# The levels of a DeltaNet scan on four 64x64 tiles of TensorE, in two PSUM banks, with two products and the turns placed elsewhere

## The reference, cut to what matters

```
a_strict = jnp.where(strict, einsum('bhnid,bhnjd->bhnij', k, k) * decay * beta[..., :, None], 0.0)
rhs = jnp.concatenate([k * (beta * jnp.exp(gc))[..., None], v * beta[..., None]], axis=-1)
sol = lax.linalg.triangular_solve(a_strict, rhs, left_side=True, lower=True, unit_diagonal=True)
```

## Time and profile before

| | us |
|---|---|
| Median of 3 runs | 4400.55 (4396.9 to 4403.37) |
| Profiled execution | 4417.49 |
| Its span in the trace | 4415.8 |
| TensorE busy, matmuls | 4001.1 (91%) |
| DVE busy | 2326.8 (53%) |
| ACT busy | 1489.9 (34%) |
| POOL busy | 608.8 (14%) |
| Granted clock of TensorE, mean | 0.96 |

### The profile page before, as it was taken

The page is one execution under the profiler, slowest core; times in us unless marked ns, Lnnn a source line. Parts: engine busy times, 40 slices in busy tenths (PEclk is TensorE's granted clock), DMA queues, the critical chain, the costliest instruction groups (busy, mean ns, idle before and its releaser), DMA issues. The chain is left out here.

```text
span 4415.8 us, 107674 instructions
## 1 busy us (share of the span) xinstructions
PE 4001.1 (91%) x46477; PEld 3548.8 (80%) x46477; DVE 2326.8 (53%) x4078; ACT 1489.9 (34%) x2670; POOL 608.8 (14%) x755
## 2 busy tenths in 40 slices
PE   6999989999958888999998999989999768888998
PEld 5899977897738886899998999967997568867886
DVE  4555556454474434665556555563554564345434
ACT  4333343333252222433234333343332532223222
POOL 1221200331001100121211212100330010100000
PEclk8999999999979999999999999999999789999999
DMA  5433331000200003223223333321002000012332
GB/s 200 129 113 100 101 100 53 21 2 19 61 1 4 4 4 101 81 87 95 88 70 110 101 112 116 111 67 43 3 2 79 0 3 4 4 64 77 105 96 76
DMA packets 409088, 288.04 MB, mean 65 GB/s; under 512 B 13438, under 2 KB 366180, under 8 KB 408164
## 3 DMA queue, kind: packets, MB, share of 16 engines
q1 hardware_dynamic: 408676, 281.86, 20.9%
HBM read 270.27 MB, written 11.53 MB: 64 GB/s over the span
## 5 line engine op out<-in xcount | busy, mean ns | idle before, releaser
L793 ACT ACTIVATE w_hi<-w_raw 128x512 fp32r<-128x512 f32 (+1 forms) x724 | 405.4, 612 | 647.9 <-POOL w_raw L777 339.5
L800 DVE TENSOR_TENSOR w_lo<-w_raw,w_hi 128x512 fp32r<-128x512 f32 (+1 forms) x724 | 478.4, 701 | 173.9 <-ACT w_hi L793 173.9
L908 PE MATMUL PS<-x_hi,w_hi 128*128 128x384 f32 x1680 | 562.3, 335 | 0.4 <-DVE hid_flat L1089 0.4
L908 PE MATMUL PS<-x_lo,w_hi 128*128 128x384 f32 x1680 | 561.3, 334 | 0.0
L908 PE MATMUL PS<-x_hi,w_lo 128*128 128x384 f32 x1680 | 561.2, 334 | 0.0
L1174 DVE SCALAR_TENSOR_TENSOR arena<-PS,mod,arena 128x256 f32<-128x256 f32 (+1 forms) x336 | 198.3, 632 | 340.7 <-PE PS L921 340.7
L1089 DVE TENSOR_TENSOR hid_flat<-hid_flat,PS 128x384 f32<-128x384 f32 (+1 forms) x454 | 246.7, 557 | 247.4 <-PE PS L908 156.0
L921 PE MATMUL PS<-hidden_hi,w_hi 128*128 128x256 f32 (+1 forms) x1232 | 341.8, 347 | 7.6 <-DVE hidden_lo L1141 5.7
L921 PE MATMUL PS<-hidden_lo,w_hi 128*128 128x256 f32 (+1 forms) x1232 | 336.8, 343 | 0.0
L921 PE MATMUL PS<-hidden_hi,w_lo 128*128 128x256 f32 (+1 forms) x1232 | 336.7, 343 | 0.0
L908 PEld LDWEIGHTS PS<-x_hi,w_hi 128*128 128x128 f32 x1680 | 315.4, 188 | 0.7 <-DVE hid_flat L1089 0.7
(11 more groups left out here) (361 smaller groups left out, 8360.1 us busy)
## 6 DMA issues: line engine op xcount, KB each, us to landing
w_raw<-in_ffn_w_dram SPq DMA_DIRECT2D x512, 256.0 KB, 4.0
arena<-in_ada_w_dram SPq DMA_DIRECT2D x120, 512.0 KB, 5.9
arena<-in_w_in_dram SPq DMA_DIRECT2D x64, 512.0 KB, 4.0
arena<-in_ada_w_dram SPq DMA_DIRECT2D x6, 2048.0 KB, 14.0
arena<-in_w_out_dram SPq DMA_DIRECT2D x16, 512.0 KB, 3.8
h_save<-arena SPq DMA_DIRECT2D x16, 384.0 KB, 2.5
arena<-h_save SPq DMA_DIRECT2D x2, 3072.0 KB, 14.7
w_raw<-in_ffn_w_dram SPq DMA_DIRECT2D x32, 128.0 KB, 2.3
```

Source lines behind the costliest of these rows:

```text
L793: nc.scalar.activation(w_hi[:, high_place(n, what, j), 0:size], w_raw[:, load_of[what] % 2, place, 0:size], ACT.Copy).then_inc(w_high_read ...
L800: nc.vector.tensor_tensor(w_lo[:, b, place, 0:size], w_raw[:, b, place, 0:size], w_hi[:, high_place(n, what, j), 0:size].bitcast(F32), ALU ...
L908: mm = pe.matmul(PS[:, 4 * b + bank, 0:half], w[wo], x_split[xo][:, j, k, 0:half], start=(k == 0 and q == 0), stop=(k == KH - 1 and q == 2))
```

## The change

- `times` and the product of the lower part go through `FOUR_TILES`: the order of heads is 0, 2, 1, 3, each with both halves. Heads 0 and 1 land where they did. Heads 2 and 3 land in the other half of the partitions (`lands`), so that their matmuls use the two off-diagonal 64x64 tiles of the array. Two swaps in a level bring X back to its own half.
- A group's result lies in two banks, 256 columns per head (`two_banks`, `level_blocks`): heads 0 and 1 in the first, 2 and 3 in the second. The product of the lower part goes to banks 4g and 4g + 1, the turn of X and the product with TP to 4g + 2 and 4g + 3. The last turn of X isn't spread over four tiles and goes to bank 4g + 2.
- Since bank 4g + 3 is now used in the levels, DVE's product with `begc` (AV) moves in front of all levels, directly behind ATTN of the same group, and the first turn of X waits for ATTN and AV.
- The order in a level is now, for each group, the turn of X and then the lower part times X; then for each group X times TP. The turn had been the last phase of a level.
- Before the first turn TensorE does five matmuls of 128x128 on the identity into a bank that nobody reads (`keep_busy`), and two more before the first turn of group 1.

```diff
--- before.py
+++ after.py
@@ -1595,10 +1595,6 @@
             v = t.rearrange(f"{axes} (b s j) -> {axes} b s j", s=2, j=1 << l)
             return v[:, :, :, 0, :] if axes == "p u" else v[:, :, 0, :]
 
-        def packed(t, l):
-
-            return t.rearrange("p (u b j) -> p u b j", u=4, j=1 << l)
-
         def blocks(b, p=slice(0, P)):
             return PS[p, b, 0:256].rearrange("p (u t) -> p u t", u=DN_H)
 
@@ -1715,13 +1711,27 @@
                 with pool.Fori(1 if first == 0 else 0, steps) as i:
                     step(first, a, w, i, True)
 
+
+
+
+        ACROSS = {0: HALVES[1], 64: HALVES[0]}
+        FOUR_TILES = [(u, p) for pair in ((0, 2), (1, 3)) for u in pair for p in HALVES]
+
+        def lands(u, p):
+            return p if u < 2 else ACROSS[p.start]
+
+        def two_banks(b, w):
+            return PS[:, b:b + 2, :].rearrange("p a c -> p (a c)").rearrange("p (u c) -> p u c", u=DN_H)[:, :, 0:w]
+
+        def level_blocks(b, l):
+            return two_banks(b, 32).rearrange("p u (b j) -> p u b j", j=1 << l)
+
         def pe_dn(pe, layer):
 
             def times(b, width, lhs, rhs):
 
-                for u in range(DN_H):
-                    for p in HALVES:
-                        mm = pe.matmul(PS[p, b, u * width:(u + 1) * width], lhs(u, p), rhs(u, p), start=True, stop=True)
+                for u, p in FOUR_TILES:
+                    mm = pe.matmul(two_banks(b, width)[lands(u, p), u], lhs(u, p), rhs(u, p), start=True, stop=True)
                 return mm
 
             def spread_gates(it):
@@ -1769,29 +1779,50 @@
                         turn(4 * g, DM[g]).then_inc(at_turned[g], 1)
                     n = LEVELS_DN - 1
                     xs, ts, yt = XS * layer + n * (first + i), TS * layer + n * (first + i), y_count(layer, first + i)
-                    for l in range(n):
-                        if l > 0:
-                            for g in range(2):
-                                c = 4 * g
-                                pe.wait_ge(x_ready[g], xs + l)
-                                for u in range(DN_H):
-                                    for p in HALVES:
-                                        mm = pe.matmul(packed(PS[p, c + 1, 0:128], l)[:, u], AT[g][p, u, p],
-                                                       even(XP[g][p, u, :], l, "p"), start=True, stop=True)
-                                mm.then_inc(tx_summed[g], 1)
-                            for g in range(2):
-                                c = 4 * g
-                                pe.wait_ge(tx_masked[g], ts + l)
-                                pe.wait_ge(y_ready[g], yt + l)
-                                if l == 1:
-                                    pe.wait_ge(attn_ready[g], it + 1)
-                                times(c + 2, 32, lambda u, p: YP[g][p, u, :], lambda u, p: TP[g][p, u, :]).then_inc(xd_summed[g], 1)
+                    def turn_x(g, l):
+                        pe.wait_ge(x_ready[g], xs + l + 1)
+                        if l == 0:
+                            pe.wait_ge(attn_ready[g], it + 1)
+                            pe.wait_ge(kst_ready[g], own + 1)
+                        if l < n - 1:
+                            mm = times(4 * g + 2, 64, lambda u, p: XP[g][p, u, :], lambda u, p: id_c[p])
+                        else:
+                            for u in range(DN_H):
+                                for p in HALVES:
+                                    mm = pe.matmul(blocks(4 * g + 2, p)[:, u], XP[g][p, u, :], id_c[p], start=True, stop=True)
+                        mm.then_inc(x_turned[g], 1)
+
+                    def lower_times_x(g, l):
+                        pe.wait_ge(x_ready[g], xs + l)
+                        if l == 1:
+                            pe.wait_ge(at_moved[g], it + 1)
+                        for u, p in FOUR_TILES:
+                            mm = pe.matmul(level_blocks(4 * g, l)[lands(u, p), u], AT[g][p, u, p],
+                                           even(XP[g][p, u, :], l, "p"), start=True, stop=True)
+                        mm.then_inc(tx_summed[g], 1)
+
+                    def x_times_lower(g, l):
+                        pe.wait_ge(tx_masked[g], ts + l)
+                        pe.wait_ge(y_ready[g], yt + l)
+                        times(4 * g + 2, 32, lambda u, q: YP[g][q, u, :], lambda u, q: TP[g][q, u, :]).then_inc(xd_summed[g], 1)
+
+
+
+                    def keep_busy(g, times):
+                        for _ in range(times):
+                            pe.matmul(PS[:, 4 * g + 1, 0:P], ident[:, :], ident[:, :], start=True, stop=True)
+
+                    keep_busy(0, 5)
+                    for l in range(1, n):
                         for g in range(2):
-                            c = 4 * g
-                            pe.wait_ge(x_ready[g], xs + l + 1)
-                            if l == 0:
-                                pe.wait_ge(at_moved[g], it + 1)
-                            times(c, 64, lambda u, p: XP[g][p, u, :], lambda u, p: id_c[p]).then_inc(x_turned[g], 1)
+                            if l == 1 and g == 1:
+                                keep_busy(1, 2)
+                            turn_x(g, l - 1)
+                            lower_times_x(g, l)
+                        for g in range(2):
+                            x_times_lower(g, l)
+                    for g in range(2):
+                        turn_x(g, n - 1)
                     lo, hi = HALVES
                     for g in range(2):
                         for u in range(DN_H):
@@ -1854,10 +1885,10 @@
                             if l > 0:
                                 act.wait_ge(xd_summed[g], TS * layer + n * (first + i) + l)
                             if l < n - 1:
-                                ins = sc.activation(YP[g], blocks(4 * g), ACT.Copy)
+                                ins = sc.activation(YP[g], two_banks(4 * g + 2, 64), ACT.Copy)
                             else:
                                 for p in HALVES:
-                                    ins = sc.activation(Y[g][p, :, p], blocks(4 * g, p), ACT.Copy)
+                                    ins = sc.activation(Y[g][p, :, p], blocks(4 * g + 2, p), ACT.Copy)
                             ins.then_inc(y_ready[g], 1)
                     lo, hi = HALVES
                     for g in range(2):
@@ -1907,22 +1938,20 @@
                         dve.wait_ge(kq_ready[g], it + 1)
                         dve.wait_ge(at_turned[g], it + 1)
                         v.tensor_tensor(ATTN[g], DMT[g], bank(4 * g + 2), ALU.mult).then_inc(attn_ready[g], 1)
+                        u = slice(g * DN_H, (g + 1) * DN_H)
+                        row = lambda t: bc(t[:, bass.ds(first + i, 1), u].rearrange("p o u -> p (o u)"), 2, [P, DN_H, P])
+                        dve.wait_ge(ks_ready[g], it + 1)
+                        v.tensor_tensor(AV[g], bank(4 * g + 3), row(begc), ALU.mult).then_inc(kst_ready[g], 1)
                     for l in range(1, n):
                         for g in range(2):
                             dve.wait_ge(tx_summed[g], TS * layer + n * (first + i) + l)
-                            v.tensor_tensor(TP[g].rearrange("p u (b j) -> p u b j", j=1 << l), packed(PS[:, 4 * g + 1, 0:128], l),
+                            v.tensor_tensor(TP[g].rearrange("p u (b j) -> p u b j", j=1 << l), level_blocks(4 * g, l),
                                             level_mask(l), ALU.mult).then_inc(tx_masked[g], 1)
                         for g in range(2):
                             dve.wait_ge(xd_summed[g], TS * layer + n * (first + i) + l)
                             dve.wait_ge(x_turned[g], XTS * layer + n * (first + i) + l)
                             x = even(XP[g], l)
-                            v.tensor_tensor(x, x, packed(PS[:, 4 * g + 2, 0:128], l), ALU.subtract).then_inc(x_ready[g], 1)
-                        if l == 1:
-                            for g in range(2):
-                                u = slice(g * DN_H, (g + 1) * DN_H)
-                                row = lambda t: bc(t[:, bass.ds(first + i, 1), u].rearrange("p o u -> p (o u)"), 2, [P, DN_H, P])
-                                dve.wait_ge(ks_ready[g], it + 1)
-                                v.tensor_tensor(AV[g], bank(4 * g + 3), row(begc), ALU.mult).then_inc(kst_ready[g], 1)
+                            v.tensor_tensor(x, x, level_blocks(4 * g + 2, l), ALU.subtract).then_inc(x_ready[g], 1)
                     for g in range(2):
                         hi = HALVES[1]
                         dve.wait_ge(tx_summed[g], TS * layer + n * (first + i) + n)
@@ -2422,8 +2451,6 @@
                 with pool.Fori(0, pairs) as i:
                     for q in range(2):
                         chunk(first + 2 * i + q, q, [a + 2 * i + q for a in at])
-
-        ACROSS = {0: HALVES[1], 64: HALVES[0]}
 
         def pe_rw(pe, layer):
             n = LEVELS_RW
```

## The result

The changed kernel took 4429.99 us (median of 7 runs, 4423.97 to 4442.26). The kernel before took 4406.96 us beside it (7 runs, 4396.9 to 4413.9). The ratio over all runs is 1.0059, with a 95% interval of 1.0043 to 1.0075: slower by some 26 us (23 between the two medians). The forecast was 4402, no change, with a range that ended at 4414. It was wrong.

The account below looks back on a forecast made before the run. TensorE, busy 91% of the span, was taken as the bound, with instruction arrival taking back the levels' gain: 12 steps x 0.1 us = 1.2 us, moving the median from 4400.55 to 4402 us; range for 8 in 10, 4386 to 4414.

Parts of the forecast that it names:

- Four tiles halve the time of a pair; a level without another limit takes 1.9 us.: DeltaNet levels: 15 ns a pair against 29, a level 1.9 us against 3.03, saving 4.5 us over four levels.
- The first turn waits for AV and starts at 873.3, 1.5 us into the step.: Ahead of the levels: first turn at 873.3 instead of 872.49; without other limits, the second group's next turn 0.25 us late.
- the last rival: In the levels: the four tiles don't overlap, levels stay at 3 us, +8 us, 4409 in all; chance 0.04.
- Arrival of instructions takes the gain back.: In the levels: TensorE gets only 126 pairs per 3.91 us, so a step ends 0.1 us later than before.
- The clock stays up, and the work behind the levels doesn't change.: Behind the levels: the 128x128 products ask for fewer than 9 pairs a microsecond and aren't held; no cost added.
- The filling.: Ahead of the first turns: TensorE, free at 871.94, fills the wait for AV with 5 + 2 matmuls, 14 pairs.
- The clock rival: New stops in the levels: clock falls, 3.4 us at half speed cost 1.7 us a step, say 4416; chance 0.12.

Follow-up runs that it names:

- e2_two_tiles: The changed kernel with every product of the levels on two tiles, all else as changed; ratio to the kernel before 1.0046.
- e7_no_fill: The changed kernel without the seven 128x128 matmuls on the identity ahead of the first turns; ratio to the kernel before 1.0030.
- e10_transposes_no_fill: The changed kernel with each group's turn of X as two 128x128 transposes, without the seven identity matmuls; ratio to the kernel before 1.0079.
- e11_two_tiles_no_fill: The changed kernel with every product of the levels on two tiles and without the seven identity matmuls; ratio to the kernel before 1.0008.
- e4_av_ahead: The kernel before with only AV moved ahead of the levels and the first turn waiting for it; ratio to the kernel before 1.0100.
- e1_wide: The changed kernel with two more 128x128 matmuls on the identity in each level; 4418.98 us, ratio to the kernel before 1.0025.

## Why the prediction was wrong, point by point

- **Four tiles halve the time of a pair; a level without another limit takes 1.9 us.** Right: 1.93 us (3280.90 to 3282.83). The 29 ns of a pair on two tiles come to 28 by the working given ((1.01 - 0.13) us over 31 pairs), which changes nothing.
- **The first turn waits for AV and starts at 873.3, 1.5 us into the step.** Right: 873.62, 1.54 us into a step that starts at 872.08 (the forecast's 873.3 is 1.53 behind 871.77). The price of the whole rearrangement was put at 0.7 us a step in the last rival; it was 1.1 (e2_two_tiles).
- **Arrival of instructions takes the gain back.** Right in kind: waits for issue of 0.2 to 1.8 us, one to four a step, with 3.4 to 4.4 us between the ends of neighbouring ones, and 64 more pairs cost 2.1 us. The term was mis-sized by 0.6 us a step: a clean step is 36.79 us, not 37.38, because the levels of before had some 1.5 us of slack. By this term alone the kernel would have come out 6 us faster than before. The 2048 instructions of store of the Trainium skill (Runtime: NRT & Kernel Launch, Instruction fetch mechanics) would have held a level block whole; the stops every 3.4 to 4.4 us don't agree with that.
- **The clock stays up, and the work behind the levels doesn't change.** This is the step that failed. The sum ended with the levels: of the 128x128 products it said only that they ask for few instructions and aren't held, and it had no term for the clock. The last turn, the last level and the products took 26.7 us more over ten steps, all of the loss. The clock that falls in the new stops stood as a rival with 0.12, priced at 3.4 us of half clock and 1.7 us a step. The falls came in eight of the ten steps, lasted 12.4 us on average (99.0 / 8), and made a fallen step 3.8 us longer than a clean one (40.60 against 36.79). The price rested on the one fall of the earlier trace rows, 3.4 us long, and on one such fall a step at most. Seven of the eight falls here last three to five times as long. All seven lie over most of the last turn and the last level (five begin in the levels, two just behind them), and three reach the products; the eighth, of 3.4 us, stayed within the levels, and its step (36.63 us) lost nothing. That a fall can last longer stood in the trace of the kernel before. This fall of 20.48 us lies in another stage (busy time by stretch, columns as above):

```profile
3467.67:3488.15 20.48, 13.46 (x24) 5.11 (x24) 8.66 (x10) 14.60 (x23) 0.00 (x0) 0.50 0.00 0
```

Two arguments were held against the rival: that a stretch of that length would hold 100 pairs, and that other stretches of the RWKV stage with 126 pairs in 4 us show 1.00. Neither held here: the 3.41 us ahead of the fall of 881.1 held 112 pairs, and blocks of 126 pairs every 3.4 to 4.4 us came with a fall in eight of ten steps.
- **The filling.** The forecast let it fill the wait for AV. It did prevent the fall at that pause (in e7_no_fill all ten steps fall there, in the changed kernel none does), but the clock then falls at the next stop, further back, so that more than half of the half clock (55.7 us of 99.0) lies in the middle part and the products. That cost more than the 139.9 us of e7_no_fill, of which 20.2 lie behind the levels.
- **The rest.** The clock rival named the place in part ("into the 128x128 products behind the levels"): 6.1 us were lost there, 20.6 in the last turn and the last level. Products without half clock take 16.86 us in every kernel here, so nothing else changed there.

What stays open: what decides whether the clock falls in a step, and how long it then stays low. Stops of the same kind gave a fall in eight of ten steps and none in two, a stretch with less work than those ahead of the falls kept its clock (1.63 us of 3.41), and no run here varied the stops one at a time.

## What to carry to other kernels

Making the small matmuls of a latency-bound block faster can turn a TensorE that is always busy into one that stops, and the clock may answer with half speed for 10 to 20 us (here 10.2 to 20.5 in most falls), which the work behind the block pays. Before speeding up such a block, ask what arrives next (here instructions), how long the new stops are, and which stage would be running if the clock fell there. Where instructions are the limit, try fewer of them: two 128x128 transposes for 16 small pairs took 0.6% off this kernel, where the same instructions on more tiles added 0.6%.

## What the runs showed of the hardware that I had not expected

- Granted clock at half for up to 17.1 us in one go beside single waits of 0.9 to 1.8 us (the changed kernel), and for up to 20.5 us in the ten steps behind two waits of 1.1 and 0.4 us (e10_transposes_no_fill). Such a wait isn't enough for a fall: steps with waits of 1.62 and 1.13 us kept 1.00 (the clean ones of the changed kernel). One wait of 1.1 us with nearly full levels behind it gave none (e11_two_tiles_no_fill).
- Half clock cost 0.44 to 0.50 us per microsecond behind the levels (the changed kernel), 0.41 in levels on two tiles (e4_av_ahead), 0.34 in the levels with transposes (5.2 for 15.4, e10_transposes_no_fill), and about 0.1 in levels that wait for instructions (1 to 1.4 for 13.7, e7_no_fill).
- Adding work to a kernel that stops made it faster (e1_wide against the changed kernel, 1.0025 against 1.0059), and taking filling away made it faster too (1.0030), by moving the fall to where it costs little.
- Four 64x64 tiles at 1.2 GHz keep the pace of two at 2.4 GHz (a level in 3.07 against 3.03 us).
